# Sparse and window attention in five lanes instead of three, and a new written order for two stages

## What is computed

```python
for l in range(DEPTH):
    h = x @ w_cols
    ...
    o_gla = _gla_mixer(gq, gk, gv, gg, galr, gla_w_a2[l], gla_b_a[l], gla_ln_w[l], gla_ln_b[l])
    ...
    o_rwkv = _rwkv7_mixer(rr, rk, rv, rwlr, ralr, rglr, ...)
    o_nsa = _nsa_mixer(h_nsa, pos, nsa_pos_k[l], nsa_pos_v[l], nsa_wk1[l], nsa_wk2[l], ...)
    mix = jnp.concatenate([o_gla, o_rwkv, o_nsa], axis=-1) @ w_out[l]
    x = _layer_norm(DEEPNORM_ALPHA * x + mix, ln1_w[l], ln1_b[l])
```

## Time and profile before

| | |
|---|---|
| median of three runs | 2303.24 us |
| the profiled execution | 2306.09 us, its span 2304.3 us |
| granted TensorE clock, mean | 0.981 |
| PE busy, share of the span | 2211.7 us, 96% |
| PE weight load | 1948.8 us, 85% |
| DVE | 1529.1 us, 66% |
| ACT | 1108.2 us, 48% |
| POOL | 422.3 us, 18% |
| DMA | 310.31 MB, mean 135 GB/s |
| stage b0, first to last matmul | 1245.9 to 1575.1 us |
| stage b1 | 1776.8 to 2097.5 us |

### The profile page before, as it was taken

How to read it: one execution, slowest core, us unless ns; L and a number is a source line. 1 busy time by engine, 2 the same in 40 slices (tenths; PEclk the granted TensorE clock), 3 DMA queues, 4 the chain that set the end, 5 groups by cost and what they waited for, 6 DMA issues and landing times.

```text
span 2304.3 us, 36385 instructions
## 1 busy us (share of the span) xinstructions
PE 2211.7 (96%) x14214; PEld 1948.8 (85%) x14214; DVE 1529.1 (66%) x2717; ACT 1108.2 (48%) x2003; POOL 422.3 (18%) x377
## 2 busy tenths in 40 slices
PE   6999999999999999999999998999998999999997
PEld 5888888988888888999888886888887987788886
DVE  5975765587678667766875685356766686456665
ACT  4654454365455443545554423246555533345554
POOL 2521001122122100012210140101213122001223
PEclk9999999999999999999999998899999999999999
DMA  6555432255555543134555411214554320203552
GB/s 239 194 176 163 150 125 76 81 192 180 188 190 188 178 150 118 45 103 152 192 168 184 135 49 40 83 37 147 190 186 142 134 84 20 103 28 119 187 179 93
DMA packets 88732, 310.31 MB, mean 135 GB/s; under 512 B 9840, under 2 KB 12144, under 8 KB 88048
## 3 DMA queue, kind: packets, MB, share of 16 engines
q1 hardware_dynamic: 88272, 305.29, 40.2%
q10 hardware_dynamic: 288, 2.69, 0.3%
HBM read 306.89 MB, written 1.05 MB: 134 GB/s over the span
## 4 chain that ended last, share of the span: by engine, by line
PE 91%; DVE 5%; ACT 2%; issue 1%; POOL 0%; DMA 0%; SPq 0%; DVEq 0%; ACTq 0%; POOLq 0%
PE ps L140 89%; DVE scratch L165 2%; PE ps L145 2%; ACT w_hi L154 1%; DVE w_lo L165 1%; DVE scratch L192 1%; ACT scratch L154 1%; DVE x L165 0%; POOL scratch L165 0%; DVE stats L182 0%; DMA ring<-in_w 0%; DVE scratch L177 0%; ACT scratch L191 0%; ACT h L154 0%; DVE scratch L204 0%
## 5 line engine op out<-in xcount | busy, mean ns | idle before, releaser
L165 DVE TENSOR_TENSOR w_lo<-ring,w_hi 128x1024 fp32r<-128x1024 f32 (+2 forms) x571 | 695.1, 1231 | 417.9 <-ACT w_hi L154 412.2
L140 PE MATMUL ps<-h,w_hi 128*128 128x512 f32 (+1 forms) x2784 | 871.5, 372 | 25.4 <-DVE h L177 18.6
L154 ACT ACTIVATE w_hi<-ring 128x1024 fp32r<-128x1024 f32 (+2 forms) x571 | 581.6, 1032 | 491.2 <-PE ps L140 484.1
L140 PE MATMUL ps<-h,w_lo 128*128 128x256 f32 x2448 | 686.8, 281 | 0.0
L140 PEld LDWEIGHTS ps<-h,w_hi 128*128 128x128 f32 x2784 | 505.0, 190 | 125.9 <-issue 22.7
L140 PEld LDWEIGHTS ps<-h,w_lo 128*128 128x128 f32 x2448 | 465.0, 190 | 0.0
L140 PE MATMUL ps<-f,w_hi 128*128 128x512 f32 (+1 forms) x1444 | 419.9, 357 | 3.1 <-DVE f L165 3.1
L140 PE MATMUL ps<-f,w_lo 128*128 128x256 f32 x1184 | 332.1, 280 | 0.0
L165 POOL TENSOR_TENSOR f<-f_work,f 128x256 fp32r<-128x256 f32 x132 | 187.6, 1422 | 591.5 <-ACT f L154 591.4
L140 PEld LDWEIGHTS ps<-f,w_hi 128*128 128x128 f32 x1444 | 255.6, 190 | 45.8 <-DVE w_lo L165 3.5
L140 PE MATMUL ps<-scratch 128*128 128x128 f32 (+9 forms) x1952 | 260.1, 303 | 8.3 <-DVE scratch L165 3.9
(11 more groups left out here) (136 smaller groups left out, 2210.6 us busy)
## 6 DMA issues: line engine op xcount, KB each, us to landing
ring<-in_w SPq DMA_DIRECT2D x520, 512.0 KB, 3.4
ring<-in_w SPq DMA_DIRECT2D x48, 384.0 KB, 3.5
ring<-in_w SPq DMA_DIRECT2D x16, 396.0 KB, 5.5
stage_consts<-in_ctwo ACTq DMA_DIRECT2D x1, 1344.0 KB, 5.8
stage_consts<-in_cthree ACTq DMA_DIRECT2D x1, 1281.0 KB, 5.4
ring<-in_w SPq DMA_DIRECT2D x9, 128.0 KB, 3.0
stage_consts<-in_cone SPq DMA_DIRECT2D x1, 1083.0 KB, 5.7
x<-in_x SPq DMA_DIRECT2D x4, 256.0 KB, 4.9
```

Of the source, the lines that this page charges most:

```text
L140: return self.e.matmul(out, lhsT, rhs, start=start, stop=stop, skip_group_check=free)
L154: return self.e.activation(out, x, func, **k)
L165: return self.e.tensor_tensor(out, a, b, op)
```

## The change

Three lines give the attention five lanes: two more pairs of buffers at G+4096 and G+4864, five strips of statistics, and five chains u v w a b. The words of b0 and b1 are new. The words of the other stages stay.

```diff
--- before.py
+++ after.py
@@ -38,16 +38,16 @@
 
 
 WEAVE = {
-    "b0": ("zzzzzzzzzzrrrrrrglrzzrzhgghhzhzzzzzzrzrhzzzzzzzzzzzzzzzzzhzzzzzzzzzzzzzhzzzzzzzzzzzzrhzzzzzzzhzh"
-           "rhhlzzzzzzrzzhrrhrgszzzzzzzhrzzzzhzshzzlhshrzszzhshrrhzznzzzzzzzzzzzzzzzzrzrzzzzzzzzzzzznzzznzzz"
-           "zzzzzzzznnzznznnrvzznrrrnzzzzrwzzzzzzszzrzzzzrnzzzzvwrzzzzzzzzzzszzzzzzzzzrzzznrzrsrnzursnuzrszz"
-           "zzzzrnnsuwvwsrsvsrurrrzwuzvzrururvzrvmwruwvuruvwrvwzrzvzzzuwzuuvzwvzuwwvuuwzvzumzwummmzzzzzmzzzz"
-           "zmmmmmmzzmzmmmzmmmmzzmzzzmzmmzmmzzzzzzzzzzmmmzzzzmzzmzzmzzmzzzzmmzz"),
-    "b1": ("zzzzzzzzzrzrrrrzrgghzgrrhhhzlzzzzzzzzrzhzzzzzzzrhgzzhzhzzzzzzzzzzzrzzzzzrhhlrhzrzrzhrlzzzzzhhrzr"
-           "zzzzzzzszzzzzzhzzzzzzhzrzrszzzrzhszzzhsshzrsrhrhzrzzhzzzzzzzzzzzszzzrzzzzzzzznzrzsznrsnrznzzzzzz"
-           "znzznzzwzrzzzzzznzzzznrzzsrzrnzrszrzzsrznwzzzzzzzzzzzzzzsrzzrzznvzzzzszzzzzzzzzzruzzzzzzzrzzznzz"
-           "znnrzvrnrnrwuzrurwurvuwvumrvuvrvzwrzzzzzzzzvuwuuzvwvuwwvuuwvvzuwwvuuzwzvumwummzmzmzzmmmmmmzzzmmz"
-           "zmmmzzmzmmmmmzzmmzmmzmzzmmzzzmzzmmzzzmzzmzz"),
+    "b0": ("zzzzzzzzzzzzzrrrrrrglrzzrzhgghhhzzzzzzrzrhzzzzzzzzzzzzzzzzzhzzzzzzzzzzzzzzzzzzhzzzzzzzrhzzzzzzzh"
+           "zhrhhlzzzzzzrzzhrrhrgszzzzzzhrhshzzlzzzzshzhzrzzszhshrrhzznzzzzzzzzzzzzzzrzrzzzzzzzzzzzzznnzzzzz"
+           "zzzzzzzzzzzznnzznznnrvzznrrrnzzzzrwzzzzzzszzrzzzzrnzzzzvwrzzzzzzzzszzzzzzzzzzrnrrsrnzzuzrsnuzrsz"
+           "zzzzzrnnsaubvsrsuasrrrrzwbzvzrarurwzrbmvrauwbrvaurwubrzvzzzzazwbvzauzwbvauwbzazumzbummmzzzzzmzzz"
+           "zzmmmmmmzzmmmzmzmmmmzzmzzzmzmmzmmzzzzzzzzzzmmzzzzmmzzmzzmzzmzmzzzmzz"),
+    "b1": ("zzzzzzzzzrrrrrzrgghzgrrzhhhlzzzzzzzzzrzhzzzzzzrhgzzzzzhzzzzzhzzzzzzzzzzrzzzzzzzrhhlrhzrzrzhrlzzz"
+           "zzhhrzrzzzzzzzszzzzzzhzzzzzzhzrzrszzrzhzszzzzzzhsshzrsrhrhzrzzzhzzzzzzzzzzszzzrzzzzzzzznzrzsznrs"
+           "nrznzzzzzzznzznzzwzrzzzzznzzzznrzzsrzrnzrszrzzsrznwzzzzzzzzzzzzzzzzsrzzrzznvzzzzzzzszzzzzrzzzzzu"
+           "zzzrzzznzzznnrurnrnrvazrurbvramuwbvrauwrbzvrzzzzzzzzauwbvazuwbvauwbvauwbvauwbaumbummzmzzzzmzmmzm"
+           "mzmmzzzmmzzmmmzmmzmmmmmzzmzmmzmzzzzzzzmzmmzzzzmmzmzzzmzzz"),
     "c0": ("zzzzzzzzzpppzzzzpzzzzzzzzzzzzzzzzzzzzzzzzzzzzzzzzzzzzzzzzzzzpzpazcbacdbzacdbdozozzzozoozoozzozoo"
            "zzzzzzozozzzzzzzzzzzozzzzzzzzz"),
     "c1": ("zzzzzpppzzzpzzzzzzzzzzzzzzzzzzzzzzzzzzzzzzzzzzzzzzzzzzppazbdazbcdabcdcozzoozozozzooozozzzoozzzzz"
@@ -2045,7 +2045,7 @@
         self.gate = K.area(G + 8080, 48, t=2, n=24)
         self.gate4 = self.gate.rearrange("p t (h a) -> p t h a", h=8)
         self.kk = self.kv[:, :, 0:768].rearrange("p t (a g d) -> p t a g d", a=6, g=2)
-        bufs = [(K.area(o, 384), K.area(o + 384, 384)) for o in (G + 1024, G + 6144, G + 8128)]
+        bufs = [(K.area(o, 384), K.area(o + 384, 384)) for o in (G + 1024, G + 6144, G + 8128, G + 4096, G + 4864)]
         ok = (np.arange(15) * 16 + 31)[None, :] <= np.arange(256)[:, None]
         lay = lambda m: m.reshape(2, 128, 15).transpose(1, 0, 2).reshape(128, 30)
         self.neg, self.val = (K.const(n, lambda I, m=m: lay(m), 30, area).rearrange("p (t c) -> p t c", t=2)
@@ -2055,10 +2055,10 @@
         if l == 0:
             self.causal = K.const("causal", lambda I: causal_mask(I)[:, 0:128], 128, area)
         rows = lambda h: slice(64 * (h % 2), 64 * (h % 2) + 64)
-        self.A_ = Attn(K, (stage, "n"), 3, lambda u: self.qT[rows(u // 2), u // 4, :],
+        self.A_ = Attn(K, (stage, "n"), 5, lambda u: self.qT[rows(u // 2), u // 4, :],
                        lambda u: self.kT[1 + u % 2][rows(u // 2), u // 8, :],
                        lambda u, k: self.kk[:, k, 2 * (1 + u % 2) + 1, :, :].rearrange("p g d -> p (g d)"), 64,
-                       "causal", bufs, [K.st[:, 64 + 8 * i:72 + 8 * i] for i in range(3)],
+                       "causal", bufs, [K.st[:, 64 + 8 * i:72 + 8 * i] for i in range(5)],
                        lambda u: [K.at("evicted", ((stage, "nqT"), u // 8)), K.at("evicted", ((stage, "nkT", 1 + u % 2), 0))],
                        lambda u: [], lambda u: 64 * (u // 8))
 
@@ -2082,7 +2082,7 @@
                 "l": some("np", 3),
                 "n": ([("nq", 0)] + some("nqT", 2) + some("nk", 4)
                       + [("nc", (i, s)) for i in range(2) for s in range(3)] + some("nS", 3)),
-                **lanes("A", 16, 3, "uvw"),
+                **lanes("A", 16, 5, "uvwab"),
                 "m": some("ms", 2) + [("out", (0, 0)), ("out", (1, 0))] + [("mT", 2), ("mT", 3)]
                 + ln_pieces(self.stage, [[("out", (j // 4, 1))] if j % 4 == 0 else [] for j in range(8)])}
 
```

## The result

The kernel after takes 2313.54 us (median of nine runs, 2309.57 to 2321.88), the kernel before beside it 2303.58 us (2302.44 to 2305.74): a ratio of 1.0039, interval 1.0031 to 1.0048. The prediction was 2300.6 us, with 2296.5 to 2306.0 as range and 0.05 for slower. It missed by 13 us, on the wrong side. Timed again in another set, after took 2312.99 us and before 2304.12 us, ratio 1.0045 (1.0031 to 1.0058).

The account below looks back on a forecast made before the run. PE, busy 96% of the span, was taken as the bound. Attention -0.9, fill between b1's transposes -1.5 and fill ahead of the attention -0.2 gave -2.6 us: 2303.5 us profiled, 2300.6 us median, range 2296.5 to 2306.0.

Parts of the forecast that it names:

- What bounds the kernel: Whole kernel: PE is busy 96% of the span; more lanes could take at most 7.5 us from the attention.
- Buffers and statistics: Attention of b0 and b1: five buffers by themselves add no wait and no instructions, 0 us.
- Fill in the attention: Attention: b0 keeps 15 fill letters, b1 goes from 15 to 11, 0.9 us less.
- the 1.5 named as a sign: Attention of b1: expected 1.5 us shorter, as evidence that the forecast holds.
- The waits that end: Waits before rS(1,0) in b0 and for unit 15's exponents in both stages vanish, together 0.7 us gained.
- The wait that grows: Attention of b0: 11.0 waits about 0.7 us for ACT to read rO1's bank, plus 0.7 us.
- Rival B: Clock falls more often, ahead of nk and behind rO1 in b0, 1.5 us each: 2306.6 us, chance 0.15.
- Fill between the transposes, -1.5: Output product of b1: four fills between mT2 and mT3 keep the clock at 2.4 GHz, 1.5 us less.
- Fill ahead of the attention: Before the attention: b0 some 8 fills fewer, 0.7 us gained; b1 10 more, 0.5 us lost; together -0.2 us.
- fills missing from the trace: Sign of being wrong: fills written in the words do not appear in the trace.
- Fill at the end of b1, 0: End of b1: five more fills before f5 cost 0, since f5's first product waits for x anyway.
- a difference in another stage: Sign of being wrong: the time difference lies in stages other than b0 and b1.

Follow-up runs that it names:

- k1: Kernel before with five pairs of buffers in both stages, still three chains and both old words: ratio 1.0010.
- k13: k10 with rP(1,1), rS(1,0) and rS(1,1), 20 full products, between nS1 and nS2 in b1: b1 328.10 us, ratio 1.0009.
- k10: Kernel before with ri(1,5) moved between nS1 and nS2 in b0, and four fills instead of one ahead of mT3 in b1: 2300.49 us, ratio 0.9984.
- k5: Kernel before with three more fills between mT2 and mT3 of b1, four instead of one: ratio 0.9997.
- k7: Kernel after with b0's values first and scores 6.0 behind rS(1,0), and b1's old fills ahead of its attention: ratio 1.0004.
- k4: Kernel after with values 0.2, 2.2, 1.2 ahead of scores 3.0 and 4.0 at the head of b0's attention: 2305.08 us, ratio 1.0004.
- k6: Kernel after with b0's attention starting 0.2, 3.0, 2.2, 1.2 and scores 4.0 later, one score product in the half-clock stretch: ratio 0.9999.

## Why the prediction was wrong

**What bounds the kernel.** Right: PE is full with three lanes, and no more than some microseconds of fill and waits could go. The masks of neighbouring units in b1 are 2.16 us apart as in the earlier trace rows, and the 8.0 of the new word waits 0.38 us for DVE's product, as 7.1 did in the earlier trace rows:

```profile
2048.43 0.92 PE L140 MATMUL ps<-scratch 64*128 64x128 f32 x4 [0.38 <-DVE scratch L165]
2049.28 0.38 PE L140 MATMUL ps<-mask_r 128*128 128x256 f32 x1
2051.44 0.39 PE L140 MATMUL ps<-mask_r 128*128 128x256 f32 x1
```

**Buffers and statistics, 0.** Right by the profile (k1: b0 +0.04, b1 +0.27 us); k1's ratio is 1.0010 with an interval of 1.0000 to 1.0020, so the times alone don't rule out a cost of some us.

**Fill in the attention.** Right: 30 fill matmuls in b0 and 22 in b1, where the earlier trace rows have 30 and 28.

```profile
L140 PE MATMUL ps<-consts 128*128 128x128 f32 x30 | 5.4, 278 | 0.0
...
L140 PE MATMUL ps<-consts 128*128 128x128 f32 x22 | 3.3, 288 | 0.0
```

From nS1 to the output product b1 gained 0.74 us, against the 1.1 that the terms gave for it and the 1.5 named as a sign. That is no more than the 1.5 us by which the old word itself varies there with the length of its stretch at half clock.

**The waits that end.** Wrong in b0. The step counted PE work between rP(1,1) and rS(1,0), 2.2 us instead of 1.0, and took the wait as covered. What ends it is an instruction of DVE, and the new pieces put their own instructions of DVE ahead of it: 0.79 us instead of none. The wait before 15.1 did go.

**The wait that grows.** Right: 11.0 waits 0.56 us for ACT (0.7 forecast), and its four fills are paid.

```profile
1528.22 0.92 PE L140 MATMUL ps<-scratch 64*128 64x128 f32 x4 [0.56 <-ACT scratch L154]
```

**The clock in b0.** The step that failed, by omission. The sum took PE work at one price. The earlier trace rows gave 0.97 for the attention of b0, and that number was the end of a stretch at 1.2 GHz from 1481.9 to 1488.7, which reaches into the very head that the new word reorders; I did not cut the stretch into windows, and so 3.2 us of 4.7 had no term. Rival B had the kind of mechanism (the clock) and its sign, but put it ahead of nk and behind rO1. Ahead of nk the clock of after does fall 3.4 us earlier (1396.5 instead of 1400.0), but nS2 is reached at the same time, and behind rO1 nothing changed. It priced a fall at 1.5 us by the earlier trace rows, and let it decide only with a second new fall. There was no new fall: the old one got longer, by 6.8 us at half clock, and this cost 3.2 us. The skill's section "HAM oscillation — how this bites in real kernels" (Trainium skill, "TensorE: Matmul & The Clock Gate") explains falls by idle time of PE between groups of matmuls, in its example waits for DMA of 3 to 5 us. In the earlier trace rows the trace agrees in kind, with 1.88 us idle in front, and so does k13 with its 2.0 us, both shorter than those waits. Behind nS2 it does not agree: PE shows no idle time there, and the clock falls behind thin work and not behind a gap, as k10 shows by putting full products between the two thin pieces.

**Fill between the transposes, -1.5.** Right in mechanism; 1.14 us measured, since two fills came in that I had not counted (k5 alone: 1.50 us).

**Fill ahead of the attention.** b0: -0.7 forecast, 0.0 measured up to nS2 (232.75 against 232.76 us). The count was wrong as well. From the start of b0 to nS1 the trace has, before and then after:

```profile
L140 PE MATMUL ps<-consts 128*128 128x128 f32 x346 | 46.1, 283 | 0.0
```

```profile
L140 PE MATMUL ps<-consts 128*128 128x128 f32 x316 | 41.7, 283 | 0.0
```

That is 15 fills fewer and not 8, although the words have 197 and 198 letters z up to nS2: more of the written fills found no bank. The prediction had named fills missing from the trace as a sign of being wrong. The fills that went turned into idle time, the end of the bounds that I had not taken: outside the attention PE idles 24.3 us in b0 (333.80 - 307.85 less 57.80 - 56.12) where it idled 20.8. b1: +0.5 forecast within 0 to 1.3. Up to nS1 nine profiles with the old fills and lanes take 232.1 to 233.5 us, mean 232.7; nine with the new ones 232.6 to 235.0, mean 234.1: +1.3 us with as much scatter. k7, with the old fills ahead of the new attention, took 233.20 us, as the old ones.

**Fill at the end of b1, 0.** Right: b1 is 1.0 us longer behind out(1,1) and f5 1.07 us shorter.

In sum the profiles have b0 +4.7, b1 and f5 together -0.3, and f4 +3.4, the last not of the change, though a difference in another stage was also named as a sign. At equal pace of f4 that is 4.4 us more, where 2.6 less was forecast.

**What stays open.** The medians differ by 9 to 10 us, twice, and the profiles account for 4.4 at equal paces. The long stretch in b1 stands in three of the 16 executions of after by their granted clock, at 10.7 us each, and does not move a median. The other 13 have 0.978 to 0.980, as the first profile with 0.978, so the rest is not more time at half clock. The paces of f4 and f5, 2 to 3.5 us each, move a median if one kernel draws the slow one more often. It would fit: after took 2313.76 us with both slow, which is its median, and before 2302.08 with both fast and 2306.09 with f5 slow, beside medians of 2303.24 to 2306.87. But whether after draws the slow pace more often isn't shown, since a run without a profile doesn't tell its paces. What the times do show is that most of the difference goes with the order at the head of the attention of b0: with the values first there and the rest of after unchanged, the ratio is 1.0004 in place of 1.0039 (k4), and with one piece of scores moved 0.9999 (k6). Why the times move by some 8 us there where the profiles show 3.2 has no cause here.

## What to carry to other kernels

Cut the clock into windows of a few microseconds over the whole stretch that a change reorders, before counting anything: a stretch at half clock has its own price list, and what stands in it decides how long it lasts. Behind a run of thin products put full ones whose data are there, weighted values before score products; that was worth 3.2 us for one letter moved in b0, and cost 5.5 us in b1, where the data were not there. Two lanes more were worth nothing in the orders tried, on an engine that was already full. Count the fills in the trace and not in the word. When a piece is moved to cover a wait, count what it puts on the engine that ends the wait, not only on the one that waits.

## What the runs showed that I had not expected

- A gate phase of 512- and 256-column products at full clock and without idle time runs at one of two paces, 346.7 or 353.3 ns for a pair, held for the whole phase in f4 and f5 and different there between executions of the same program.
- The clock fell behind thin products without any idle time of PE (fall at 1481.9 in before), and in the five profiles with 12 full ones between nS1 and nS2 and values behind them it did not fall.
- Once at half clock, b0 stayed there for 6.8, 10.2 or 13.7 us with none, one or two pieces of 64-row score products in the stretch, at 1.6 us of loss for each step, while 16 full products of 128 rows left it at 6.8 us and cost 1.8 us, their time at full clock; in rare executions of b1 the clock stayed at half for 30.7 us with PE busy, for 10.7 us of loss.
